# First MLP product with the weight blocks as the stationary operand and the activations as the moving one

## The reference, cut to what matters

```python
x = x + merged @ w_out[layer]
h2 = rms_norm(x, g_mlp[layer])                                     # (256, 2048)
x = x + jnp.square(jax.nn.relu(h2 @ w_mlp_in[layer])) @ w_mlp_out[layer]   # 2048 -> 8192 -> 2048
return rms_norm(x, g_final)
```

## Time and profile before

| | |
|---|---|
| median of 3 runs | 1688.63 us (1688.58 to 1689.73) |
| the profiled execution: time, span | 1688.95 us, 1687.2 us |
| PE busy, matmuls | 1666.1 us (99%), 7806 |
| PEld busy | 1388.2 us (82%) |
| DVE busy, ACT busy | 996.4 us (59%), 840.6 us (50%) |
| granted TensorE clock, mean | 0.997 of full speed |
| mean traffic | 180 GB/s |
| the four MLP groups | about 962 to 1675 us of the span |

### The profile page before, as it was taken

How to read it: one execution, slowest core, us unless ns; L and a number is a source line. 1 busy time by engine, 2 the same in 40 slices (tenths; PEclk the granted TensorE clock), 3 DMA queues, 4 the chain that set the end, 5 groups by cost and what they waited for, 6 DMA issues and landing times.

```text
span 1687.2 us, 22042 instructions
## 1 busy us (share of the span) xinstructions
PE 1666.1 (99%) x7806; PEld 1388.2 (82%) x7806; DVE 996.4 (59%) x1194; ACT 840.6 (50%) x1149; POOL 61.5 (4%) x58
## 2 busy tenths in 40 slices
PE   8999999999999999999999999999999999999997
PEld 7888888888888888888888888888888888888885
DVE  5776677776666678864565554544445445444453
ACT  5665456555555455543445454434543454335543
POOL 0000000000000141200000000000000000000000
PEclk9999999999999999999999999999999999999999
DMA  8655656555566654456565766666666665666563
GB/s 234 178 155 155 174 162 174 166 157 158 167 189 184 197 152 138 138 177 196 177 230 181 221 184 184 191 194 188 181 191 193 195 183 183 195 193 185 185 195 117
DMA packets 198450, 303.61 MB, mean 180 GB/s; under 512 B 14576, under 2 KB 70496, under 8 KB 198240
## 3 DMA queue, kind: packets, MB, share of 16 engines
q1 hardware_dynamic: 198192, 302.40, 59.6%
q10 hardware_dynamic: 176, 0.07, 0.0%
HBM read 300.33 MB, written 2.10 MB: 179 GB/s over the span
## 4 chain that ended last, share of the span: by engine, by line
issue 58%; PE 37%; DVE 4%; POOL 1%; DMA 0%; ACT 0%; SPq 0%; ACTq 0%; POOLq 0%
PE G L1228 11%; PE G L1229 11%; PE G L1230 11%; PE S L1236 1%; DVE wlo L715 1%; PE S L1352 1%; DVE prob L1011 1%; POOL q_rs L1144 0%; PE S L1335 0%; PE S L1339 0%; PE S L1357 0%; DMA raw<-in_w_in 0%; PE S L1345 0%; DVE pT_lo L1016 0%; PE S L1311 0%
## 5 line engine op out<-in xcount | busy, mean ns | idle before, releaser
L439 ACT ACTIVATE whi<-raw 128x1024 fp32r<-128x1024 f32 x560 | 593.4, 1060 | 762.9 <-PE G L1230 732.7
L715 DVE TENSOR_TENSOR wlo<-raw,whi 128x1024 fp32r<-128x1024 f32 x560 | 681.5, 1224 | 456.2 <-ACT whi L439 455.9
L1228 PE MATMUL G<-whi,a_hi 128*128 128x512 f32 x1472 | 580.3, 394 | 2.1 <-DVE wlo L715 2.1
L1229 PE MATMUL G<-wlo,a_hi 128*128 128x512 f32 x1472 | 574.0, 390 | 0.0
L1230 PE MATMUL G<-whi,a_lo 128*128 128x512 f32 x1472 | 573.8, 390 | 0.0
L1228 PEld LDWEIGHTS G<-whi,a_hi 128*128 128x128 f32 x1472 | 276.8, 188 | 59.0 <-DVE wlo L715 1.6
L1230 PEld LDWEIGHTS G<-whi,a_lo 128*128 128x128 f32 x1472 | 276.7, 188 | 58.5
L1229 PEld LDWEIGHTS G<-wlo,a_hi 128*128 128x128 f32 x1472 | 276.8, 188 | 55.6
L1228 PE MATMUL G<-whi,b_hi 128*128 128x512 f32 x640 | 250.8, 392 | 0.7 <-issue 0.7
L1230 PE MATMUL G<-whi,b_lo 128*128 128x512 f32 x640 | 249.4, 390 | 0.0
L1229 PE MATMUL G<-wlo,b_hi 128*128 128x512 f32 x640 | 249.2, 389 | 0.0
(11 more groups left out here) (182 smaller groups left out, 959.5 us busy)
## 6 DMA issues: line engine op xcount, KB each, us to landing
raw<-in_w_in SPq DMA_DIRECT2D x136, 512.0 KB, 3.9
raw<-in_w_mlp_in SPq DMA_DIRECT2D x128, 512.0 KB, 3.8
raw<-in_w_mlp_out SPq DMA_DIRECT2D x128, 512.0 KB, 4.5
raw<-in_w_in SPq DMA_DIRECT2D x72, 256.0 KB, 3.3
raw<-in_w_in SPq DMA_DIRECT2D x144, 128.0 KB, 3.5
raw<-in_w_ssm_up SPq DMA_DIRECT2D x32, 512.0 KB, 3.8
raw<-in_w_attn_up SPq DMA_DIRECT2D x32, 512.0 KB, 4.6
raw<-in_w_out SPq DMA_DIRECT2D x32, 512.0 KB, 4.6
```

What stands on the lines that cost most here:

```text
L439: act.activation(whi[:, slot, 0:width], raw[:, slot, 0:width], ACT.Copy).then_inc(hi_made, 1)
L715: dve.tensor_tensor(wlo[:, slot, 0:width], raw[:, slot, 0:width], whi[:, slot, 0:width].bitcast(F32), ALU.subtract).then_inc(lo_made, 1)
L1228: pe.matmul(out_ap, hi[:, k, cols], w_hi, start=start, stop=False)
L1229: pe.matmul(out_ap, hi[:, k, cols], w_lo, start=False, stop=False)
```

## The change

The product `mlp_in` swaps its operands. A 128x128 block of weights is stationary and the activations move. `b_hi` and `b_lo` are now two halves of one tensor `b_both`, so that for one block of the contraction the hi part and the lo part of all 256 tokens are 512 consecutive columns. For each block k and each group c of 128 hidden columns there are two matmuls: `whi` against hi and lo together (512 columns), and `wlo` against hi (256 columns), added to the first half of the same bank. The result has hidden columns on the partitions, four banks for a window: even windows in G, odd windows in S. It needs no transposes.

The side work `hidden` becomes: at p = 0 ACT copies the second halves (whi·lo) out of PSUM (128x1024), DVE adds the first halves, then takes the maximum with 0 and multiplies by the row scale, at p = 1 ACT squares in place, at p = 2 ACT copies to `a_hi` and DVE subtracts to `a_lo`. The row scale is needed along the free axis now; two small matmuls against the identity at p = 6 of the first `mlp_in` window spread it over all partitions, and ACT copies it to `rstd_row`. As `mlp_in` uses all four banks of G or S, the last `out` window and the odd `mlp_out` windows have their results in S.

```diff
-    b_hi = place("b_hi", [P, KT, T], F32R)
-    b_lo = place("b_lo", [P, KT, T], F32R)
+    b_both = place("b_both", [P, KT, 2, T], F32R)
+    b_hi, b_lo = b_both[:, :, 0, :], b_both[:, :, 1, :]
...
@@ ACT, residual @@
+            if p == 7 and j == 3:
+                act.wait_ge(row_mm, 1)
+                act.activation(rstd_row[:, :], S[:, 2, 0:T], ACT.Copy).then_inc(hid_hi, 1)
...
@@ ACT @@
         def hidden(p, idx, pr, pp):
             g, j = idx
             if p == 0:
                 act.wait_ge(used, done(pr, pp))
-                act.wait_ge(rstd_x, 2)
-                for tb in range(TB):
-                    last = act.activation(tmp_a[:, tb, :], product(pp, tb), ACT.Relu,
-                                          scale=rstd_mlp[:, tb:tb + 1])
-                last.then_inc(taken[pp], 1)
-                act.wait_ge(ts_t, g * 4 + (TS_HID + j))
-                act.wait_ge(taken[pp], pr + 1)
-                act.activation(tmp_b[:, :, :], tmp_a[:, :, :], ACT.Square).then_inc(hid_sq, 1)
+                act.activation(hidden_t, hidden_banks(j)[:, :, T:2 * T], ACT.Copy).then_inc(hid_t, 1)
+            if p == 1:
+                act.wait_ge(hid_v, g * 4 + (j + 1))
+                act.activation(hidden_u, hidden_u, ACT.Square).then_inc(hid_sq, 1)
             if p == 2:
-                split_high(g * 4 + (TS_HID + j), a_hi, 4 * j)
+                act.wait_ge(hid_sq, g * 4 + (j + 1))
+                act.activation(a_hi[:, 4 * j:4 * j + 4, :], hidden_u, ACT.Copy).then_inc(hid_hi, 1)
...
@@ DVE @@
         def hidden(p, idx, pr, pp):
             g, j = idx
+            if p == 0:
+                dve.wait_ge(hid_t, g * 4 + (j + 1))
+                dve.wait_ge(hid_hi, g * 4 + (j + 1))
+                dve.tensor_tensor(hidden_u, hidden_t, hidden_banks(j)[:, :, 0:T], ALU.add).then_inc(taken[pp], 1)
+                dve.wait_ge(taken[pp], pr + 1)
+                dve.scalar_tensor_tensor(out=hidden_u, in0=hidden_u, scalar=0.0,
+                                         in1=rstd_row[:, :].unsqueeze(1).to_broadcast([P, 4, T]),
+                                         op0=ALU.max, op1=ALU.mult).then_inc(hid_v, 1)
             if p == 2:
-                split_low(g * 4 + (TS_HID + j), a_hi, a_lo, 4 * j)
+                dve.wait_ge(hid_hi, g * 4 + (j + 2))
+                dve.tensor_tensor(a_lo[:, 4 * j:4 * j + 4, :], hidden_u,
+                                  a_hi[:, 4 * j:4 * j + 4, :].bitcast(F32), ALU.subtract).then_inc(hid_lo, 1)
...
@@ PE @@
+        def weights_first(bank, k, w_hi, w_lo):
+            pe.matmul(bank, w_hi, b_both[:, k, :, :].rearrange("p h t -> p (h t)"), start=(k == 0), stop=False)
+            return pe.matmul(bank[:, 0:T], w_lo, b_hi[:, k, :], start=False, stop=(k == KT - 1))
...
-        def hidden(p, idx, pr, pp):
-            g, j = idx
-            if p == 1:
-                pe.wait_ge(hid_sq, g * 4 + (j + 1))
-                split_round(g * 4 + (TS_HID + j), lambda c, tb: tmp_b[:, tb, c * P:(c + 1) * P])
@@ PE, residual @@
+            if p == 6 and j == 3:
+                pe.wait_ge(rstd_x, 2)
+                for tb in range(TB):
+                    last = pe.matmul(S[:, 2, tb * P:(tb + 1) * P], rstd_mlp[:, tb:tb + 1].to_broadcast([P, P]),
+                                     ident[:, :], start=True, stop=True)
+                last.then_inc(row_mm, 1)
...
+                if p == 0 and kind == "mlp_in" and idx[1] == 1:
+                    pe.wait_ge(hid_hi, 1)
...
+                    if kind == "mlp_in":
+                        for c in range(4):
+                            last = weights_first(hidden_banks(idx[1])[:, c, :], k,
+                                                 whi[:, p % RING, kk * N + c * P:kk * N + (c + 1) * P],
+                                                 wlo[:, p % RING, kk * N + c * P:kk * N + (c + 1) * P])
+                        continue
```

More of the change, by code:

```diff
@@ L64 @@
 U_END = U_MLP + 32
-TS_X, TS_Z, TS_MERGED, TS_X2, TS_HID = 0, 4, 8, 12, 16
+TS_X, TS_Z, TS_MERGED, TS_X2, TS_END = 0, 4, 8, 12, 16
 def walk(eng, window):
@@ L253, in build @@
     fin = place("fin", [P, TB, D])
+    rstd_row = place("rstd_row", [P, T])
     keep = ExitStack()
@@ L295, in build @@
         sem(n) for n in ("at_hi", "at_lo", "at_pt_lo", "r_lo", "r_cross")]
-    merge_v, hid_sq, fin_v, fin_a = sem("merge_v"), sem("hid_sq"), sem("fin_v"), sem("fin_a")
+    merge_v, fin_v, fin_a = sem("merge_v"), sem("fin_v"), sem("fin_a")
+    hid_t, hid_v, hid_sq, hid_hi, hid_lo = [sem(n) for n in ("hid_t", "hid_v", "hid_sq", "hid_hi", "hid_lo")]
+    row_mm = sem("row_mm")
     CONV_V = 4 * TAPS + 1
@@ L307, in product, with late_product, out_product, hidden_banks @@
         return G[:, 2 * par + tb, :]
+    def late_product(par, tb):
+        return (S if par else G)[:, tb, :]
+    def out_product(j, tb):
+        return S[:, 2 + tb, :] if j == 3 else product(j % 2, tb)
+    def hidden_banks(j):
+        return S if j % 2 else G
     def x_bank(j, c, part=slice(0, T)):
@@ L312, in x_bank @@
         return bank[:, c // 2, c % 2 * T + part.start:c % 2 * T + part.stop]
+    hidden_t = tmp_a[:, :, :].rearrange("p b (c t) -> p (b c) t", c=2)
+    hidden_u = tmp_b[:, :, :].rearrange("p b (c t) -> p (b c) t", c=2)
     u_dt = tmp_a[:, :, :].rearrange("p b n -> p (b n)")[:, 0:6 * TB * DTW].rearrange(
@@ L1064, in merged, with add_product @@
                 split_low(j + TS_MERGED, a_hi, a_lo, j * 4, factor=0.5)
-        def add_product(j, pr, pp):
+        def add_product(j, pr, pp, bank):
             dve.wait_ge(used, done(pr, pp))
@@ L1070, in add_product @@
                 part = x_sb[:, j, tb, :]
-                last = dve.tensor_tensor(part, part, product(pp, tb), ALU.add)
+                last = dve.tensor_tensor(part, part, bank(tb), ALU.add)
             last.then_inc(taken[pp], 1)
@@ L1075, in residual @@
             if p == 0:
-                add_product(j, pr, pp)
+                add_product(j, pr, pp, lambda tb: out_product(j, tb))
             if p == 2:
@@ L1086, in hidden @@
             g, j = idx
+            if p == 0:
[6 more added lines that the diff above has]
+                                         op0=ALU.max, op1=ALU.mult).then_inc(hid_v, 1)
             if p == 2:
-                split_low(g * 4 + (TS_HID + j), a_hi, a_lo, 4 * j)
+                dve.wait_ge(hid_hi, g * 4 + (j + 2))
+                dve.tensor_tensor(a_lo[:, 4 * j:4 * j + 4, :], hidden_u,
+                                  a_hi[:, 4 * j:4 * j + 4, :].bitcast(F32), ALU.subtract).then_inc(hid_lo, 1)
         def add(p, j, pr, pp):
             if p == 0:
-                add_product(j, pr, pp)
+                add_product(j, pr, pp, lambda tb: late_product(pp, tb))
         def times_gain(j, tb):
@@ L1121, in _ @@
             part = x_sb[:, 3, tb, :]
-            dve.tensor_tensor(part, part, product(1, tb), ALU.add).then_inc(fin_v, 1)
+            dve.tensor_tensor(part, part, late_product(1, tb), ALU.add).then_inc(fin_v, 1)
         for tb in range(TB):
@@ L1425, in residual @@
                 split_round(TS_X2 + j, lambda c, tb: x_sb[:, j, tb, c * P:(c + 1) * P])
-        def hidden(p, idx, pr, pp):
-            g, j = idx
-            if p == 1:
-                pe.wait_ge(hid_sq, g * 4 + (j + 1))
-                split_round(g * 4 + (TS_HID + j), lambda c, tb: tmp_b[:, tb, c * P:(c + 1) * P])
-        table = {f.__name__: f for f in (rates, decays, conv, scan, zgate, rope, attend, merged, residual, hidden)}
+            if p == 6 and j == 3:
[4 more added lines that the diff above has]
+                last.then_inc(row_mm, 1)
+        table = {f.__name__: f for f in (rates, decays, conv, scan, zgate, rope, attend, merged, residual)}
         def window(r, par, kind, idx, sides):
@@ L1438, in window @@
                 pe.wait_ge(taken[par], r)
-            rounds = {"ssm_up": TS_MERGED, "out": TS_X2, "mlp_in": TS_HID}.get(kind)
+            rounds = {"ssm_up": TS_MERGED, "out": TS_X2, "mlp_in": TS_END}.get(kind)
+            ready = ts_lo
             if kind == "mlp_out":
-                rounds = idx[0] * 4 + (TS_HID + 4)
+                rounds, ready = idx[0] * 4 + 4, hid_lo
             late = (kind == "out" and idx == 0) or (kind == "mlp_in" and first(idx[0]) and idx[1] == 0) or (
                 kind == "mlp_out" and idx[1] == 0)
+            into = product
+            if kind == "out":
+                into = lambda _, tb: out_product(idx, tb)
+            if kind == "mlp_out":
+                into = late_product
             for p in range(PIECES):
@@ L1448, in window @@
                 if p == 0 and rounds is not None:
-                    pe.wait_ge(ts_lo, rounds - 1 if late else rounds)
+                    pe.wait_ge(ready, rounds - 1 if late else rounds)
+                if p == 0 and kind == "mlp_in" and idx[1] == 1:
+                    pe.wait_ge(hid_hi, 1)
                 if p == PIECES - 2 and late:
-                    pe.wait_ge(ts_lo, rounds)
```

(5 more changed lines are left out.)

## The result

| | before | after |
|---|---|---|
| median | 1688.58 us (5 runs) | 1696.79 us (5 runs) |
| lowest, highest | 1687.74, 1689.73 | 1696.08, 1698.67 |
| profiled execution's span | 1687.2 us | 1694.3 us |

The ratio is 1.0052, 95% interval 1.0042 to 1.0063: 8.2 us slower. Forecast were 1684.3 us and a range up to 1690.0.

The account below looks back on a forecast made before the run. PE was taken to set the time, busy 99% of the span. Transposes -14.7, pairs +9.9 and row scale +0.5 gave -4.3 us, so 1684.3 us, with a range of 1679.2 to 1690.0.

Parts of the forecast that it names:

- five rivals: Other outcomes: settled pair 1679.5, no effect 1689.0, unhidden load 1694.5, proportional cost 1674.4, DVE delaying PE 1700 for 1 us.
- Rounds of transposes: Hidden windows: 16 rounds of eight transposes on PE go, 0.92 us each, -14.7 us, all on the path.
- The pairs: `mlp_in` windows: 1024 pairs of a 512- and a 256-column matmul cost 0.3496 us each against 0.3399 before, +9.9 us.
- the band of 0.3475 to 0.352: Cost in us of a 512- and 256-column pair under the main forecast, 1682.2 to 1686.8 us, chance 0.42.
- Rival A: `mlp_in` windows: 512-column matmuls cost 0.2266 us even behind a 256, pair 0.3449, total 1679.5 us; chance 0.25.
- B's upper bound: `mlp_in` windows: a pair costs 0.3542 us, +14.6 us, so the change has no effect, 1689.0 us; chance 0.16.
- Rival C: `mlp_in` windows: the next weights' load isn't wholly hidden under a 256-column matmul; slower, 1694.5 us if 0.010 a pair; chance 0.10.
- The row scale: Two fp32 128x128 matmuls against the identity, once on PE: +0.5 us, between 0.3 and 1.0, without a wait.
- The side work at nothing: Hidden windows: added ACT and DVE work costs PE nothing; tightest slack 2 us, at DVE's split of piece 3.
- The sum: Whole kernel: -14.7 for transposes, +9.9 for pairs, +0.5 for the row scale, together -4.3 us.

## Why the prediction was wrong

**The step that failed** is one clause: "The loops' branches and the tail behind the last matmul stay as they are." I counted the instructions of a piece for their time and not for their place in the program. The code ahead of the loop grew by 72 instructions, the loop's start came to lie four instructions before the end of a fetched packet, and each of the two branches back left a gap 3.2 to 4.0 us longer than before, plus the lower clock behind it: 11.3 us by the trace, 11.1 and 11.4 by the two kernels moved out of this place, and 9.8 in the kernel before moved into it. None of the five rivals named it.

The Trainium skill has the rule behind the branch's cost, on its page "Runtime: NRT & Kernel Launch", section "Instruction fetch mechanics": programs are fetched in blocks of 16 KiB, ahead and in order only, and a taken branch to a block that is not among the two held waits for its fetch. The traces agree on the 16 KB packets and on the wait, branches of 3.3 to 4.8 us with a packet fetched in each. They don't agree on two: a loop of 527 instructions needs three packets and was not fetched again (last section), and the measurement decides. What they add is that the block's own remainder decides what is paid behind the branch.

Could it have been seen? The clue was in the trace of before. L109's branch took 4.1 us there, and PE's two waits on "issue" stood at exactly those places. I read their sum of 0.7 us as nothing. It was the uncovered end of two branches of 4.1 us, with 3.7 us of cover each.

**Rounds of transposes**, -14.7: right, -14.2 measured alone.

**The pairs**, +9.9: near in size, for the wrong reason and by luck. By the pieces of the changed kernel they cost 7 x 64 x 0.0068 + 9 x 64 x 0.0132 = 10.7 us. Both speeds lie outside the band of 0.3475 to 0.352 that the prediction named as its test; only their average lies inside. Rival A (0.3449, settled) nearly holds in seven windows, and B's upper bound (0.3542) in nine. With 12 slow windows, as in the changed kernel written out, they cost 11.9. Rival C, a 512 that starts late behind a 256 because of the load, is not what separates the two: in both a load's record starts with the running matmul and lasts 0.19 us, and of the 0.006 us between them 0.005 stand behind the 512s (0.232 to 0.237) and 0.002 behind the 256s (0.115 to 0.117).

**The row scale**, +0.5: right. Its piece was 0.36 us longer and the next 0.09.

**The side work at nothing**: right. In the window at 1006.94 DVE's split of piece 3 began at 1011.54, with piece 3 due at 1015.3, and PE waited for `wlo` nowhere in the stage. The timeline of the changed kernel's DVE there:

```profile
1009.15 1.22 DVE L1107 TENSOR_TENSOR tmp_b<-tmp_a,S 128x1024 f32<-128x1024 f32 x1 [2.46 <-ACT tmp_a L683]
1010.40 1.22 DVE L1109 SCALAR_TENSOR_TENSOR tmp_b<-tmp_b,rstd_row 128x1024 f32<-128x1024 f32 x1
1011.54 2.35 DVE L732 TENSOR_TENSOR wlo<-raw,whi 128x1024 fp32r<-128x1024 f32 x2
```

**The sum** for what I had looked at, -4.3 us, compares with -2.5 (1685.67 against 1688.16) once the loop's start is out of the bad place, and with -1.5 when both loops are written out. There the terms as measured give -14.2 + 11.9 + 0.5 = -1.8. So the direction was right for these terms, the size nearly three times too large, and most of the difference is the pairs.

## What to carry to other kernels

A change that alters the number of instructions ahead of a loop also moves the loop. Where the body is too long to be kept, each pass pays a branch of several microseconds, and how much of it shows depends on where the start lies in the fetched packets: look at the duration of the branch and at the gap behind it, move the start by a few instructions, or write the loop out. Compare two kernels with the loop written out before judging the change inside it, and read a small wait as the visible end of a cost that something covers.

## What the runs showed of the hardware that I had not expected

- Four instructions ahead of a loop moved the time by 11.4 us in 1697. The loop over the state-space windows, 527 instructions, has branches of 0.08 to 0.24 us, and no packet of PE's program was fetched between 160 and 420 us, while it ran; the MLP loop of 1688 has branches of 4.1 us. Between these sizes lies what PE keeps.

```profile
L75 PEldq COMPARE_BRANCH  x6: 76/208/244, 170.4 to 425.6; - x6
```

- A stream of alternating 512- and 256-column matmuls has two steady speeds, 0.3467 and 0.3531 us a pair, and mostly stays in the one that it starts in. One 128x128 transpose moved it from the slow to the fast one in all three places, and so did some of the gaps at the loop's turn. What sets the speed inside PE these runs don't show.
